# A hybrid decoder layer on one Trainium2 core: the FFN's down-projection as one level of Strassen's products over the whole stage

## What is computed

```python
h = rms_norm(x, norm_ffn_pre)
f = (jax.nn.silu(h @ w_ffn_gate) * (h @ w_ffn_up)) @ w_ffn_down   # (512, 5632) @ (5632, 2048)
return x + rms_norm(f, norm_ffn_post)
```

## Time and profile before

| | |
|---|---|
| median of 3 runs | 2681.66 us (2681.66 to 2681.68) |
| the profiled execution | 2682.89 us, span 2681.2 us |
| TensorE busy | 2658.6 us, 99% |
| VectorE, ScalarE, GpSimd busy | 60%, 37%, 15% |
| DMA | 368.38 MB, mean 137 GB/s |

### The profile page before, as it was taken

How to read it: one execution, slowest core, us unless ns; L and a number is a source line. 1 busy time by engine, 2 the same in 40 slices (tenths; PEclk the granted TensorE clock), 3 DMA queues, 4 the chain that set the end, 5 groups by cost and what they waited for, 6 DMA issues and landing times.

```text
span 2681.2 us, 38803 instructions
## 1 busy us (share of the span) xinstructions
PE 2658.6 (99%) x14477; PEld 2272.1 (85%) x14477; DVE 1615.2 (60%) x1957; ACT 985.4 (37%) x1291; POOL 396.0 (15%) x627
## 2 busy tenths in 40 slices
PE   8999999999999999999999999999999999999998
PEld 7888888888888888888888888888888888888887
DVE  5233332243345999942668999899999973334335
ACT  5222322232333444432534444444444433223223
POOL 3978027760000000000000000000000000000000
PEclk9999999999999999999999999999999999999999
DMA  6444563335433444542424333343433344444443
GB/s 182 139 145 128 121 181 112 99 87 168 155 120 116 168 156 134 196 178 98 149 95 139 112 119 131 110 133 110 137 105 127 123 183 178 146 147 141 145 148 134
DMA packets 262606, 368.38 MB, mean 137 GB/s; under 512 B 23696, under 2 KB 213264, under 8 KB 260464
## 3 DMA queue, kind: packets, MB, share of 16 engines
q1 hardware_dynamic: 232776, 287.89, 32.8%
q0 software_dynamic: 12448, 60.80, 7.3%
q10 hardware_dynamic: 17288, 18.40, 2.0%
HBM read 324.60 MB, written 46.60 MB: 138 GB/s over the span
## 4 chain that ended last, share of the span: by engine, by line
PE 96%; DVE 2%; issue 1%; ACT 1%; ACTq 0%; DVEq 0%
PE ps L744 26%; PE ps L750 13%; PE ps L480 8%; PE ps L484 8%; PE ps L482 8%; PE ps L792 6%; PE ps L793 6%; PE ps L794 6%; PE ps L601 2%; PE ps L603 2%; PE ps L602 2%; PE ps L587 1%; PE ps L588 1%; PE ps L586 1%; PE ps L568 1%
## 5 line engine op out<-in xcount | busy, mean ns | idle before, releaser
L468 DVE TENSOR_TENSOR w_lo<-raw,w_hi 128x1024 fp32r<-128x1024 f32 x176 | 229.7, 1305 | 541.7 <-ACT w_hi L464 541.6
L464 ACT ACTIVATE w_hi<-raw 128x1024 fp32r<-128x1024 f32 x176 | 186.4, 1059 | 560.0 <-PE ps L484 346.4
L480 PE MATMUL ps<-a_both,w_hi 128*128 128x512 f32 x640 | 252.2, 394 | 0.1
L482 PE MATMUL ps<-a_both,w_hi 128*128 128x512 f32 x640 | 249.2, 389 | 0.0
L484 PE MATMUL ps<-a_both,w_lo 128*128 128x512 f32 x640 | 249.2, 389 | 0.0
L744 PE MATMUL ps<-a_both,w_hi 128*128 128x512 f32 x872 | 216.8, 391 | 0.0
L769 DVE TENSOR_TENSOR f_lo<-f_raw,f_hi 128x512 fp32r<-128x512 f32 x84 | 58.2, 692 | 255.6 <-ACT f_hi L765 255.6
L744 PEld LDWEIGHTS ps<-a_both,w_hi 128*128 128x128 f32 x872 | 160.3, 188 | 31.0
L765 ACT ACTIVATE f_hi<-f_raw 128x512 fp32r<-128x512 f32 x84 | 53.0, 631 | 303.5 <-PE ps L794 303.4
L744 PE MATMUL ps<-a_both,w_hi_b 128*128 128x512 f32 x640 | 159.2, 391 | 0.0
L480 PEld LDWEIGHTS ps<-a_both,w_hi 128*128 128x128 f32 x640 | 120.1, 188 | 27.6 <-issue 1.8
(11 more groups left out here) (426 smaller groups left out, 6232.7 us busy)
## 6 DMA issues: line engine op xcount, KB each, us to landing
raw<-in_w_in SPq DMA_DIRECT2D x108, 512.0 KB, 4.3
raw<-in_w_ffn_gate SPq DMA_DIRECT2D x88, 512.0 KB, 4.5
raw<-in_w_ffn_down SPq DMA_DIRECT2D x88, 512.0 KB, 3.6
raw_b<-in_w_ffn_up SPq DMA_DIRECT2D x80, 512.0 KB, 5.2
f_raw<-f_d SPq DMA_DIRECT2D x88, 256.0 KB, 2.6
raw<-in_w_out SPq DMA_DIRECT2D x32, 512.0 KB, 3.5
mix_raw_b<-in_w_in SPq DMA_DIRECT2D x28, 512.0 KB, 5.9
f_d<-f_t ACTq DMA_DIRECT2D x22, 512.0 KB, 2.8
```

Of the source, the lines that this page charges most:

```text
L464: nc.scalar.activation(w_hi[:, m % 2, :], raw[:, m % 4, :], ACT.Copy).then_inc(hi_ready, 1)
L468: nc.vector.tensor_tensor(w_lo[:, m % 2, :], raw[:, m % 4, :], w_hi[:, m % 2, :].bitcast(F32), ALU.subtract).then_inc(lo_ready, 1)
L480: nc.tensor.matmul(o, wh[:, k, cols], x_hi[:, kt0 + k, :], start=first and k == 0, stop=False, skip_group_check=halves)
L482: nc.tensor.matmul(o, wh[:, k, cols], x_lo[:, kt0 + k, :], start=False, stop=False, skip_group_check=halves)
```

## The change

The down-projection becomes one level of the same seven-product scheme over the whole stage. With A the activation (tokens x 5632) and W the weights, the contraction is halved by taking even and odd tiles of a pair m (`PAIRS` = 22), tokens are halved (256 each), columns are halved (1024 each). The seven products Z6, Z7, Z5, Z4, Z1, Z3, Z2 are done one after the other, each over all 22 pairs, so there are 154 steps (`DSTEPS`) of 2 token tiles x 2 column tiles x 3 = 12 matmuls. A product fills four banks, alternately 4 to 7 and 0 to 3; Z2 goes on in the banks of Z1. The finished product's banks are read by VectorE (and once by ScalarE) beside the steps of the next one and are combined in SBUF (`y_part`, in `o_gain`); squares, gains and part of the normalisation follow beside the last products. The tail for the last two token tiles is as before. The loops of the stage are unrolled.

The sums of the weights are made in DRAM: in turn t GpSimd issues plain copies (`v_begin`) and adding transfers (`v_add`), 512 KB each, 88 of each kind in all. Turn t waits until all of the turn before has landed. Turns 0 to 3 lie in the output projection, 4 and 5 at the start of the FFN, turn 6 + m behind the store of pair m's sums. The activation's sums are made by VectorE right after `gate_times_up` (`f_pair_sums`, four subtractions of 128 x 256), in one buffer that GpSimd stores (`store_f_sums`, 512 KB).

```diff
+PAIRS = DKT // 2
+DSTEPS = 7 * PAIRS
+Z6, Z7, Z5, Z4, Z1, Z3, Z2 = range(7)
-        def load_f(sp, n, groups, kt):
+        def load_f(sp, n):
+            q, m = n // PAIRS, n % PAIRS
+            if q in (Z6, Z7, Z5, Z3):
+                sp.wait_ge(f_sums_stored, 16 * (m + 1))
+                src = fs_d[m, :, {Z5: 0, Z6: 1, Z7: 2, Z3: 3}[q], :]
+            else:
+                sp.wait_ge(f_stored[m % 2], START + 16 * (m // 2) + 16)
+                src = f_d[2 * m + (0 if q == Z1 else 1), :, quad[1 if q == Z4 else 0]]
+            sp.wait_ge(f_lo_ready, F0 + n - 3)
+            sp.dma_start(f_raw[:, n % 4, :], src).then_inc(f_in[n % 4], 16)
+        def load_down(sp, n):
+            q, m = n // PAIRS, n % PAIRS
+            if q in (Z5, Z6, Z7, Z4):
+                v = {Z5: 0, Z6: 1, Z7: 2, Z4: 3}[q]
+                sp.wait_ge(v_added, 16 * v_adds(m + (2, 4, 2, 6)[v]))
+                src = v_d[v][m]
+            else:
+                src = w_block(*{Z1: (0, 0), Z2: (1, 0), Z3: (1, 1)}[q], m)
+            sp.wait_ge(lo_ready, B_DN + n - 3)
+            sp.dma_start(raw[:, n % 4, :], src).then_inc(landed[n % 4], 16)
...
+        def piece_d(pe, n):
+            q, m = n // PAIRS, n % PAIRS
+            if m == 0:
+                down_banks_free(pe, q)
+            pe.wait_ge(lo_ready, B_DN + n + 1)
+            pe.wait_ge(f_lo_ready, F0 + n + 1)
...
+            for c in range(2):
                 toks = slice(c * P, c * P + P)
                 for d in range(2):
+                    o = down_bank(q, c, d)
...
+            def f_pair_sums(g, a):
+                f = f_t[:, a, :, :]
+                f11, f21, f12, f22 = f[:, 0, quad[0]], f[:, 0, quad[1]], f[:, 1, quad[0]], f[:, 1, quad[1]]
+                s1, s2, s3, s4 = (f_sums[:, i, :] for i in range(4))
+                dve.wait_ge(f_made, START + 2 * g + a + 1)
+                if not isinstance(g, int) or g or a:
+                    dve.wait_ge(f_sums_stored, 32 * g + 16 * a)
+                tt(s1, f21, f22, ALU.subtract).then_inc(f_sums_made, 1)
+                tt(s3, f11, f21, ALU.subtract).then_inc(f_sums_made, 1)
+                dve.wait_ge(f_sums_made, 8 * g + 4 * a + 2)
+                tt(s2, f11, s1, ALU.subtract).then_inc(f_sums_made, 1)
+                dve.wait_ge(f_sums_made, 8 * g + 4 * a + 3)
+                tt(s4, s2, f12, ALU.subtract).then_inc(f_sums_made, 1)
...
                     if not first and j % 2 == 0:
                         gate_times_up(*((g, j - 1) if j else (g - 1, 3)))
+                        f_pair_sums(*((g, (j - 1) // 2) if j else (g - 1, 1)))
...
             gate_times_up(FFG - 1, 3)
+            f_pair_sums(FFG - 1, 1)
...
+            def dve_beside(n):
+                q, i = (n - PAIRS - 1) // PAIRS, (n - PAIRS - 1) % PAIRS
+                if q == Z7 and i < 4:
+                    c, d = i // 2, i % 2
+                    dve.wait_ge(piece_done, B_DN + 2 * PAIRS)
+                    combine(AFTER_Z6 + i, y_part(2 + c, d), down_bank(Z7, c, d), y_part(c, 2 + d), ALU.subtract)
...
+                if q == Z1 and i < 12:
+                    c, d = i // 6, i // 3 % 2
+                    dve.wait_ge(piece_done, B_DN + 5 * PAIRS)
...
+            for n in range(2, DSTEPS - 4):
+                down_lo(dve, n)
+                dve_beside(n)
...
+            def v_begin(v, m, src):
+                pool.dma_start(v_d[v][m], src).then_inc(v_begun, 16)
+            def v_add(v, m, src):
+                pool.dma_start(v_d[v][m], src, accum_op=ALU.add, max_dma_last_dim=4096).then_inc(v_added, 16)
+            def v_turn(t):
+                if t:
+                    pool.wait_ge(v_begun, 16 * v_begins(t))
+                if t > 1:
+                    pool.wait_ge(v_added, 16 * v_adds(t))
+                if t < PAIRS:
+                    v_begin(0, t, w_block(0, 0, t))
+                    v_begin(2, t, w_block(0, 1, t))
+                if 1 <= t <= PAIRS:
+                    v_add(0, t - 1, w_block(0, 1, t - 1))
+                    v_add(2, t - 1, w_block(1, 1, t - 1))
+                if 2 <= t < PAIRS + 2:
+                    v_begin(1, t - 2, v_d[0][t - 2])
+                if 3 <= t < PAIRS + 3:
+                    v_add(1, t - 3, w_block(1, 1, t - 3))
+                if 4 <= t < PAIRS + 4:
+                    v_begin(3, t - 4, v_d[1][t - 4])
+                if 5 <= t < PAIRS + 5:
+                    v_add(3, t - 5, w_block(1, 0, t - 5))
+            def store_f_sums(m):
+                pool.wait_ge(f_sums_made, 4 * m + 4)
+                pool.dma_start(fs_d[m], f_sums[:, :, :]).then_inc(f_sums_stored, 16)
...
+            for m in range(PAIRS):
+                store_f_sums(m)
+                v_turn(6 + m)
             pool.wait_ge(product, PROD0 + 7 * UNITS)
             pool.dma_start(gain_o[:, :], A["norm_ffn_post"][0:1, :].partition_broadcast(P)).then_inc(gb_in[1], 16)
```

More of the change, by code:

```diff
@@ L784, in piece_d @@
+        def piece_d(pe, n):
[4 more added lines that the diff above has]
+            pe.wait_ge(f_lo_ready, F0 + n + 1)
             wh = FFN.hi[(n + 2) % 4].rearrange("p (d n) -> p d n", n=512)
             wl = FFN.lo[(n + 2) % 4].rearrange("p (d n) -> p d n", n=512)
-            for c in (2, 3, 0, 1) if n == 0 else range(CLS):
+            opens, closes = m == 0 and q != Z2, m == PAIRS - 1
+            for c in range(2):
@@ L795, in piece_d @@
-                    if last and (c < CLS - 1 or d == 0):
-                        mm.then_inc(down, 1)
+                    o = down_bank(q, c, d)
+                    nc.tensor.matmul(o, f_hi[n % 2][:, toks], wh[:, d, :], start=opens, stop=False,
+                                     skip_group_check=True)
+                    nc.tensor.matmul(o, f_hi[n % 2][:, toks], wl[:, d, :], start=False, stop=False,
+                                     skip_group_check=True)
+                    mm = nc.tensor.matmul(o, f_lo[n % 2][:, toks], wh[:, d, :], start=False, stop=closes,
+                                          skip_group_check=True)
@@ new lines, in _ @@
+            for n in range(2, DSTEPS - 4):
+                down_hi(act, n)
+                act_beside(n)
+            for k in range(4):
+                n = DSTEPS - 4 + k
+                end_split_hi(act, k, B_DN + n)
+                f_split_hi(act, n, ef_hi[:, k, :])
+            for c in range(2):
+                for d in range(2):
+                    act.wait_ge(down, 2 * c + d + 1)
+                    squared(12 + 2 * c + d, c, d, down_bank(Z2, c, d))
+                last_root(2 + c)
@@ L2513, in _, with finish_part @@
-            with dve.Fori(0, FFG - 3) as i:
-                for k in range(5, 9):
-                    down_lo(dve, DKT + k, i)
-            for k in range(2 * DKT - 7, 2 * DKT - 4):
-                down_lo(dve, k, 0)
+            def finish_part(i, h, parts):
+                c = OUT_ORDER[i]
+                cols = slice(D // parts * h, D // parts * (h + 1))
+                stt(x2_b[:, c, cols], o_gain[:, c, cols], stat[:, 2, c:c + 1], x2_b[:, c, cols], ALU.mult,
+                    ALU.add).then_inc(out_ready, 1)
@@ L2530, in _ @@
+            for i in (2, 3):
+                c = OUT_ORDER[i]
+                dve.wait_ge(ffn_sq, 13 + 2 * c)
+                gained(c, 0, down_bank(Z2, c, 0))
+                last_mean(i)
+                gained(c, 1, down_bank(Z2, c, 1))
+                finish_begin(i)
+                for h in range(4 if i == CLS - 1 else 2):
+                    finish_part(i, h, 4 if i == CLS - 1 else 2)
         @block.gpsimd
```

286 lines of the change are left out of this document (146 added, 140 removed).

## The result

| | before | after |
|---|---|---|
| median | 2681.66 us | 2716.12 us (4 runs, 2715.48 to 2719.79) |
| span of the profiled execution | 2681.2 us | 2713.6 us |
| ratio after / before | | 1.0131, 95% interval 1.0114 to 1.0149 |

The change made the kernel 34.5 us slower. I had forecast 2634 us, 47.6 us faster, in a range to 2700: wrong in sign, and outside the range.

The account below looks back on a forecast made before the run. TensorE, busy for 99% of the span, was taken as the bound. The terms -59.8 + 2 + 1.4 + 7 + 1.8 sum to -47.6 us, giving 2634 us from a median of 2681.66, range 2622 to 2700.

Parts of the forecast that it names:

- Matmuls removed: Down-projection: 264 matmuls fewer, 1848 for 2112, at 0.2267 us each, -59.8 us.
- The feeders of the down-projection: Down-projection steps of 2.72 us: loads, VectorE's splits and combinations and ScalarE's work all keep up, 0 us.
- VectorE's sums: SwiGLU units: four subtractions cost 1.8 us per pair, absorbed by 2.2 us of VectorE's idle time; 0 us, at most 6.
- The adding transfers in steady state: SwiGLU units: turns of 15.6 us bring DMA work to 31.3 of 38.93 us per pair, weights land just in time; 0 us.
- The first turns: First SwiGLU units: turns come closer together beside the units' loads, +2 us, bounds 0 and 8.
- The seam: Units to down-projection: sums delay a piece +1.4, load 6 waits behind the gain and residual fetch +7, clock dip +1.8 us.
- the same chain as before: Kernel's end: after the last matmul square, mean, root, gain, parts and store take some 7 us, unchanged, 0 us.
- A: Turns in the units: DRAM-to-DRAM bytes take the engines twice, 41.7 us wanted of 38.93 per pair; 2679 us, chance 0.05.
- C: Seam and first turns: queues share evenly, so no gap or clock dip comes and first turns hide; 2623 us, chance 0.06.
- B: Turns in the units: adds cost five plain transfers or more, sums' store queues behind, VectorE then TensorE wait; 2762 us, chance 0.19.

Follow-up runs that it names:

- the repaired kernel: Changed kernel with turns 1 to 5 early in the output projection, later ones halved and released by products, last two in the down-projection, residual and gain late: 2629.09 us.
- the late residual: Changed kernel with the gain fetched from step 30 of the down-projection and the residual in four parts at steps 36, 42, 48 and 54: 2704.35 us.

## Why the prediction was wrong

**Matmuls removed, -59.8 us: right.** 1848 ran at 0.2267 us; the stage in the repaired kernel is 425.3 us, 418.9 of it theirs.

**The feeders of the down-projection, 0: right.** Between 2400 and 2600 TensorE is busy for all of the 200 us at full clock, with the DMA engines busy for 0.75.

**VectorE's sums, 0: right alone, wrong in company.** They took 1.6 us (1870.97 to 1872.57) and cost at most 1.6 us in the whole kernel without turns. Beside the turns some 20 went with them. The prediction called 2.2 us idle in a pair free and spent 1.8 of them; it did not say that they were also what a late load would be made up from.

**The adding transfers in steady state, 0: this is the step that failed.** Its prices were near: an add costs 1.8 copies where the sum had two; q0 held the engines for 18.7 us of a pair, where the sum had 15.6 + 1.3; the other queues took 14.4, as in the sum (which used a share of 0.37; the row that it names says 0.36, 14.0 us). Its volume argument held as well: the repaired kernel moves the same in 38.97 us. What failed is the sentence "Starved until 1833 the halves land by 1836.2 and 1839.4: just in time." That was a deadline met by 0.6 us (1836.77), from a turn whose length was known to some microseconds, and I took 0 as its cost, with nothing on the upper side. The first half was read 18.87 us behind its issue (1879.89 to 1898.76) where the forecast had 16.2. The burst was longer than counted: q0 was busy for some 22.5 us from the turn's start (1873.5 to about 1896), where the forecast had 19, for the turn itself is dearer (17.3 us for 15.6), and `f_d`'s store (q10 in the rows above) and the weights take their packets in between. VectorE then waits 3 to 4 us for it (58.0 us, 15 times), with 0.4 us of idle time left to make that up. TensorE stops for 30 us in some 14 pairs, and the clock and what the stops hide come on top: 47 us. The term should have been written as a rate: each microsecond of lateness past the slack counts once per pair, 16 times or so, as I had written for the down-projection's steps and not for the units.

**The first turns, +2 (0 to 8): 29 us.** The bound was taken from the crowd of turns; the run with those moved shows that one meeting with loads that have little lead stops TensorE for 15.5 us.

**The seam, +10.2 us: right, for half the right reason.** Loads behind the burst of the residual, a gap of 2.52 and one of 5.09 us and a stretch at 0.82 to 0.89 of the clock; 11.8 us came back with the late residual. But I read the earlier trace rows, 5.08 MB against 0.62, as a queue that doesn't share, and held it against the Trainium skill ("DMA: Bandwidth & Descriptors", section "Queues, rings and completion order"), by which each engine goes round its queues packet by packet. The same rows' first column says 276 packets against 243: the queues did share by packets. The rule was right, my "even split" of bytes was not what it says, and the trace agreed with it: the queues take turns. (The Trainium skill puts some 9 to 17 descriptors into a packet there; in this trace the rows themselves alternate one for one.) Had I read the packets in those rows, a 1 KB row against rows of 4 and 32 KB would have given the weight queue a fifth or less of the bytes during every turn.

**Not in the forecast: the end.** With steps half as long, VectorE's `ef_lo` is late for the last four; TensorE stands for 0.8 + 1.6 us at 2693 to 2696, and the clock is 0.90 from 2690 to 2706.6. The repaired kernel shows the same (1.11 + 1.45 us, 0.92 from 2600 to 2620.4). That is 4 to 5 us that "the same chain as before" left out.

**The rivals.** A (copies cost double) is refuted by the packet's price: 1.15 MB in 3 us is some 380 GB/s, where half of a load's rate would be 200. C (even shares of the bytes) is refuted for rows of unequal size, and holds for equal ones. B, the one on the slower side, had the right place and engines (VectorE, then TensorE, once per pair), but let them wait for the sums' store, and made all hang on the price of an add: at two plain transfers it could not happen.

## What to carry to other kernels

A transfer that moves off the path is free only if no other queue's deadline falls into it; list the issues whose landing is waited for and lay background bursts between them, by counting the engine that sets the pace and not by the work that makes their data. During a burst each queue gets packets in equal number, so compare the row sizes of the queues to see who starves. Treat "just in time" as a loss that repeats with the loop, and idle time of a feeding engine as the reserve for late loads: whoever spends it should price both.

## What the runs showed of the hardware

- Queues share the DMA engines packet by packet, one for one, whatever the size: 98, 100 and 99 packets in 3 us with 0.75, 0.20 and 0.10 MB; 352 and 354 with equal rows.
- An adding transfer in DRAM takes 1.8 times the engines' time of a copy at rows of 4 KB (0.292 against 0.159 us a row; 2.76 against 1.57 us for 512 KB), and 0.101 us for a row of 1 KB.
- While its packets wait, the issuing queue is held too: four issues took 14.06 us inside a turn and 2.25 outside.
- DMA engines busy for 0.90 of a stretch delay nobody if the bursts miss the deadlines.
- Short stops of TensorE can cost clock too: behind five of the changed kernel's 14 stops of 1.1 to 2.6 us the granted clock fell to 0.5 for 3 to 4 us, which costs 8.5 us in 600. In the run without sums, with no stop over 1.71 us, it stayed at 1.00.
